# Both directions of a pair's inverses on four quarters of TensorE, and products of zeros in the first stretch of the mixers

## The reference

```python
h = rmsnorm(x) * (1 + sc1) + sh1;  x = x + 0.5 * gt1 * swiglu(h)
h = rmsnorm(x) * (1 + sc2) + sh2;  x = x + gt2 * mix(h)      # GLA | Hyena | RWKV-7
h = rmsnorm(x) * (1 + sc3) + sh3;  x = x + 0.5 * gt3 * swiglu(h)
```

```python
def step(state, inp):                      # one token
    r_t, w_t, k_t, v_t, a_t, b_t = inp
    sa = einsum('bhvk,bhk->bhv', state, a_t)
    state = state * w_t[:, :, None, :] + sa[..., None] * b_t[:, :, None, :] + v_t[..., None] * k_t[:, :, None, :]
    return state, einsum('bhvk,bhk->bhv', state, r_t)
```

## Time and profile before

| what | us |
|---|---|
| median of 3 executions | 2027.83 |
| lowest and highest | 2014.14, 2028.31 |
| the profiled execution | 2029.15 |
| its span, first to last instruction | 2027.2 |
| TensorE busy | 1910.2 (94%) |
| VectorE, ScalarE, GpSimd busy | 1095.8, 739.1, 33.2 |
| layer 0: first and second mixer stage | 478.7 to 600.5, 601.4 to 723.2 |
| layer 1: the same | 1459.1 to 1578.3, 1579.1 to 1695.0 |

### The profile page before, as it was taken

One profiled execution on the slowest core, in us unless ns is written; L12 is line 12 of the kernel. 1 busy time (PEld: TensorE's weight loads), 2 busy tenths in 40 slices (PEclk: granted clock), 3 DMA queues, 4 the chain that ended last, 5 costly groups with the idle time before them and its releaser, 6 DMA issues. The chain is left out here.

```text
span 2027.2 us, 38671 instructions
## 1 busy us (share of the span) xinstructions
PE 1910.2 (94%) x16360; PEld 1748.5 (86%) x16360; DVE 1095.8 (54%) x1845; ACT 739.1 (36%) x1108; POOL 33.2 (2%) x62
## 2 busy tenths in 40 slices
PE   5999999998888989999999999999978898999997
PEld 2888999995665879999999999999747497999997
DVE  3544444865537466554455554476564756655533
ACT  3333333435224244333343333344441424433322
POOL 0000000000001000000000000000000100000000
PEclk9999999998789999999999999999979798999999
DMA  7766233423446233333343333442240401333332
GB/s 271 263 224 222 90 129 137 158 101 113 142 129 212 85 109 125 124 124 113 127 145 124 124 118 114 138 169 90 87 148 4 159 13 66 125 124 124 105 128 89
DMA packets 73192, 263.25 MB, mean 130 GB/s; under 512 B 9696, under 2 KB 10848, under 8 KB 56928
## 3 DMA queue, kind: packets, MB, share of 16 engines
q1 hardware_dynamic: 73056, 261.27, 37.9%
HBM read 259.08 MB, written 2.16 MB: 129 GB/s over the span
## 5 line engine op out<-in xcount | busy, mean ns | idle before, releaser
L157 PE MATMUL ps<-h_head,w_head 128*128 128x386 f32 x1824 | 624.0, 342 | 9.2 <-DVEq L243 4.1
L157 PE MATMUL ps<-h_head,w_rest 128*128 128x386 f32 x1824 | 619.3, 340 | 0.0
L157 PE MATMUL ps<-h_rest,w_head 128*128 128x386 f32 x1824 | 617.3, 338 | 0.0
L219 ACT ACTIVATE w_head<-w_raw 128x2048 fp32r<-128x2048 f32 (+1 forms) x176 | 303.0, 1721 | 609.2 <-PE ps L157 598.9
L222 DVE TENSOR_TENSOR w_rest<-w_raw,w_head 128x2048 fp32r<-128x2048 f32 (+1 forms) x176 | 360.7, 2049 | 204.4 <-ACT w_head L219 204.3
L157 PEld LDWEIGHTS ps<-h_head,w_head 128*128 128x128 f32 x1824 | 345.9, 190 | 28.6 <-issue 18.8
L157 PEld LDWEIGHTS ps<-h_head,w_rest 128*128 128x128 f32 x1824 | 345.8, 190 | 0.0
L157 PEld LDWEIGHTS ps<-h_rest,w_head 128*128 128x128 f32 x1824 | 343.0, 188 | 0.2
L157 PE MATMUL ps<-gu_head,w_head 128*128 128x384 f32 x832 | 279.9, 336 | 11.4 <-DVE gu_rest L813 11.4
L157 PE MATMUL ps<-gu_rest,w_head 128*128 128x384 f32 x832 | 279.4, 336 | 0.0
L157 PE MATMUL ps<-gu_head,w_rest 128*128 128x384 f32 x832 | 279.3, 336 | 0.0
(11 more groups left out here) (294 smaller groups left out, 1798.1 us busy)
## 6 DMA issues: line engine op xcount, KB each, us to landing
w_raw<-in_w_in SPq DMA_DIRECT2D x88, 1024.0 KB, 4.8
w_raw<-in_w_out SPq DMA_DIRECT2D x64, 704.0 KB, 4.0
w_raw<-in_ada_w SPq DMA_DIRECT2D x41, 1024.0 KB, 6.2
ada_raw<-in_ada_w SPq DMA_DIRECT2D x31, 1024.0 KB, 6.4
w_raw<-in_mix_in SPq DMA_DIRECT2D x26, 1024.0 KB, 4.9
w_raw<-in_mix_out SPq DMA_DIRECT2D x8, 1024.0 KB, 5.0
hyena_const<-in_hconst SPq DMA_DIRECT2D x2, 1792.0 KB, 9.6
x<-in_x_in SPq DMA_DIRECT2D x1, 1536.0 KB, 12.2
```

The lines of the kernel that those rows point to most:

```text
L157: return nc.tensor.matmul(out, lhsT, rhs, start=start, stop=stop)
L219: return nc.scalar.activation(self.HI[src], self.RAW[src], ACT.Copy)
```

## The change

The inverse is built otherwise. With J for identity plus something: X2 and D2 (`s1`, for each z), then T1 = J2·T, X4, T2 = J4·T, X8, and INV = J8·T; then Q is its transpose, EX = ET·INV and G its transpose form, Y1 = JE·Q, EX2 from G and EX, and Y = JG·Y1. `crossed` issues both directions together: direction 0 writes the partitions it reads, direction 1 the other half, into two neighbouring banks, so that four quarters of the array are used, and an eviction takes both banks, 768 columns, at once. Because the halves are crossed once more by `straight`, the heads are back in place at the end. The banks of each pair change to 0, 1, 2, 3 and 4, 5, 6, 7.

`keep_busy` multiplies a tile of zeros with the identity and adds to bank 7, in the first mixer stage at three places. The orders of both stages are written anew on every engine; in the two-pair stage `B` and `A` go in step. The waits of the modulation units change: the second set's first unit waits for B's `y1` too.

The diff, cut to its core:

```diff
+                self.X, self.T = (self.XQ[:, :, :, x, :] for x in range(2))
+                self.D4, self.X4, self.J8 = self.D, self.D2, self.X
+                self.INV, self.Q, self.EX, self.JE, self.G = self.J2, self.T, self.D, self.J4, self.X
+                self.Y1, self.JG, self.Y = self.D2, self.ET, self.J4
...
+            def crossed(self, ba, bb, lhsT, rhs):
+                for c in range(NCH):
+                    for h in range(2):
+                        mm(bank(ba, TOK)[half(h), c * C:c * C + C], lhsT[half(h), 0, c, :], rhs[half(h), 0, c, :])
+                    for h in range(2):
+                        last = mm(bank(bb, TOK)[half(1 - h), c * C:c * C + C], lhsT[half(h), 1, c, :], rhs[half(h), 1, c, :])
                 return last
...
+            def straight(self, ba, bb, lhsT, rhs):
+                for z, b in enumerate((ba, bb)):
+                    for c in range(NCH):
+                        for h in range(2):
+                            last = mm(bank(b, TOK)[half(h), c * C:c * C + C], lhsT[half(h), z, c, :], rhs[half(h), z, c, :])
+                return last
...
+            def pe_d4(self, pe):
+                self.after_act(pe, "d2_1")
+                self.after_dve(pe, "x2_1")
+                self.pe_step(self.crossed(*self.even(), self.X, self.D2), "d4")
+            def pe_t1(self, pe):
+                self.after_dve(pe, "j2_1")
+                self.after_pool(pe, "q1")
+                self.pe_step(self.crossed(*self.odd(), self.J2, self.T), "t1")
+            def pe_x4(self, pe):
+                self.after_act(pe, "d4")
+                self.pe_step(self.crossed(*self.even(), self.D2, self.X), "x4")
+            def pe_t2(self, pe):
+                self.after_dve(pe, "j4")
+                self.after_act(pe, "t1")
+                self.pe_step(self.crossed(*self.odd(), self.J4, self.T), "t2")
+            def pe_x8(self, pe):
+                self.after_dve(pe, "x4")
+                self.pe_step(self.crossed(*self.even(), self.D4, self.X4), "x8")
+            def pe_t(self, pe):
+                self.after_dve(pe, "j8")
+                self.pe_step(self.straight(*self.odd(), self.J8, self.T), "t")
+            def pe_q(self, pe):
+                self.after_act(pe, "t_0")
+                self.after_dve(pe, "t_1")
+                for c in range(NCH):
+                    for h in range(2):
+                        mm(bank(self.b0, TOK)[half(h), c * C:c * C + C], self.INV[half(h), 0, c, :], cst("istack", 0, None, 64 * h, 64 * h + 64))
+                    for h in range(2):
+                        last = mm(bank(self.b1, TOK)[half(1 - h), c * C:c * C + C], self.INV[half(h), 1, c, :],
+                                  cst("istack", 0, None, 64 * h, 64 * h + 64))
+                self.pe_step(last, "q")
+            def pe_ex(self, pe):
+                self.after_act(pe, "t_0")
+                self.after_dve(pe, "t_1")
+                self.pe_step(self.crossed(*self.odd(), self.ET, self.INV), "ex")
+            def pe_g(self, pe):
+                self.after_act(pe, "q")
+                self.pe_step(self.crossed(*self.even(), self.INV, self.ET), "gm")
+            def pe_y1(self, pe):
+                self.after_act(pe, "q")
+                self.after_dve(pe, "ex")
+                self.pe_step(self.crossed(*self.odd(), self.JE, self.Q), "y1")
+            def pe_ex2(self, pe):
+                self.after_act(pe, "gm")
+                self.after_dve(pe, "ex")
+                self.pe_step(self.crossed(*self.even(), self.G, self.EX), "ex2")
...
+            def pe_y(self, pe):
+                self.after_dve(pe, "jg")
+                self.after_act(pe, "y1")
+                self.pe_step(self.straight(*self.even(), self.JG, self.Y1), "y")
...
+            def act_both(self, act, name, out, banks):
+                self.after_pe(act, name)
+                self.act_step(nc.scalar.activation(out, self.both(banks), ACT.Copy), name)
+            def act_d4(self, act):
+                self.after_pool(act, "q1")
+                self.act_both(act, "d4", self.D4, self.even())
...
+            def dve_one_plus(self, dve, product, out, banks, name):
+                self.after_pe(dve, product)
+                ones = cst("istack").unsqueeze(1).unsqueeze(1).to_broadcast([128, 2, NCH, C])
+                self.tt(out, self.both(banks), ones, ALU.add, name)
+            def dve_one_plus_x4(self, dve):
+                self.dve_one_plus(dve, "x4", self.J4, self.even(), "j4")
+            def dve_x4(self, dve):
+                self.after_pe(dve, "x4")
+                self.dve_step(nc.vector.tensor_copy(self.X4, self.both(self.even())), "x4")
...
-                A = Pair(scope, SEMS[0:5], lay, 0, (0, 1, 2), 6, PR, TG, AL, MO)
-                G = Gla(scope, SEMS[5:10], lay, (3, 4, 5), P, MO)
+                A = Pair(scope, SEMS[0:5], lay, 0, (0, 1, 2), 3, PR, TG, AL, MO)
+                G = Gla(scope, SEMS[5:10], lay, (4, 5, 6), P, MO)
                 ADA = Ada(scope, SEMS[10:15], 2, [7] * sets, 1)
                 bias_done = SEMS[15]
+                zero = sb(scope, "zero", [128, 128])
+                def keep_busy(pe, n):
+                    A.after_pool(pe, "identity")
+                    for _ in range(n):
+                        mm(bank(7, 128), zero[:, :], cst("ident"), False, False)
...
+                    keep_busy(pe, 9)
                     ada_products(pe, 0, 4)
                     A.pe_nat(pe, 1)
                     ada_products(pe, 0, 5)
+                    keep_busy(pe, 7)
                     A.pe_gram(pe, 0, 0)
                     ada_products(pe, 0, 6)
+                    keep_busy(pe, 5)
...
-                A = Pair(scope, SEMS[0:5], lay, 1, (0, 1, 2), 6, PR, TG, AL, MO)
-                B = Pair(scope, SEMS[5:10], lay, 2, (3, 4, 5), 6, PR, TG, AL, MO, (A.act_done, A.AC["s6_1"]))
+                A = Pair(scope, SEMS[0:5], lay, 1, (0, 1, 2), 3, PR, TG, AL, MO)
+                B = Pair(scope, SEMS[5:10], lay, 2, (4, 5, 6), 7, PR, TG, AL, MO, (SEMS[16], 1))
...
+                            pe.wait_ge(B.act_done, B.AC["y1"])
```

More of the change, by code:

```diff
@@ L1492, in pe_gram, with even, odd, both @@
                 self.pe_step(last, f"gram{z}{b}")
-            def each(self, b, lhsT, rhs):
-                for c, e in PROBS:
-                    last = mm(bank(b, TOK)[half(e), c * C:c * C + C], lhsT(c, e), rhs(c, e))
-                return last
-            def power(self, z):
-                return lambda c, e: self.XQ[half(e), z, c, 0, :]
-            def q(self, z):
-                return lambda c, e: self.XQ[half(e), z, c, 1, :]
-            def of(self, buf, z):
-                return lambda c, e: buf[half(e), z, c, :]
+            def crossed(self, ba, bb, lhsT, rhs):
[4 more added lines that the diff above has]
+                        last = mm(bank(bb, TOK)[half(1 - h), c * C:c * C + C], lhsT[half(h), 1, c, :], rhs[half(h), 1, c, :])
+                return last
+            def straight(self, ba, bb, lhsT, rhs):
[4 more added lines that the diff above has]
+                return last
+            def even(self):
+                return self.b0, self.b1
+            def odd(self):
+                return self.b2, self.b3
+            def both(self, banks):
+                ba, bb = banks
+                assert bb == ba + 1
+                return PS[:, ba * 512:bb * 512 + 512].rearrange("p (z x) -> p z x", x=512)[:, :, 0:TOK].rearrange("p z (c t) -> p z c t", t=C)
+            def one_of(self, banks, z):
+                return bank(banks[z], TOK).rearrange("p (c t) -> p c t", t=C)
             def pe_s1(self, pe, z):
-                ba, bb = self.pair_banks(z)
                 self.after_act(pe, "bt12")
@@ new lines, in pe_s1 @@
+                for b, lhsT, rhs in ((ba, self.X, self.D), (bb, self.D, self.X)):
+                    for c in range(NCH):
+                        for h in range(2):
+                            last = mm(bank(b, TOK)[half(h), c * C:c * C + C], lhsT[half(h), z, c, :], rhs[half(h), z, c, :])
+                self.pe_step(last, f"s1_{z}")
+            def pe_d4(self, pe):
+                self.after_act(pe, "d2_1")
+                self.after_dve(pe, "x2_1")
+                self.pe_step(self.crossed(*self.even(), self.X, self.D2), "d4")
@@ L1818, in dve_power_q @@
-            def dve_power_q(self, dve, z):
-                ba, bb = self.pair_banks(z)
-                self.after_pe(dve, f"s2q_{z}")
-                spans = [(0, ba, 2)] if bb == ba + 1 else [(0, ba, 1), (3, bb, 1)]
-                for first, b, n in spans:
-                    products = PS[:, b * 512:b * 512 + n * 512].rearrange("p (b x) -> p b x", b=n)[:, :, 0:TOK]\
-                        .rearrange("p b (c x t) -> p b c x t", c=3, x=2)
-                    xq = self.XQ[:, z, first:first + 3 * n, :, :].rearrange("p (b c) x t -> p b c x t", b=n)
-                    nc.vector.tensor_copy(xq[:, :, :, 0, :], products[:, :, :, 0, :])
```

(9 more changed lines are left out.)

580 lines of the change are left out of this document (262 added, 318 removed).

## The result

The changed kernel takes 2038.9 us (median of 7 runs, 2037.5 to 2045.9), the kernel before 2020.9 in seven runs beside it (2014.1 to 2028.3): a ratio of 1.0081, interval 1.0063 to 1.0099. It is slower by 0.8%, and 25 us above the forecast of 2014. The profiled executions took 2037.51 us (span 2035.7) and 2029.15; they are 8.4 us apart where the medians are 18.

The account below looks back on a forecast made before the run. Bounds: TensorE in inverses and chunk loops, VectorE early in the two-pair stage, a falling clock early in the first stage. 2029.15 - 8.5 - 2.7 - 3.0 = 2015.0, less 1.3 for the median: 2014 us; range 2000 to 2032.

Parts of the forecast that it names:

- a crossed step of both directions (48 records) is 0.98 us: Inverse on four quarters: 20.5 ns a record, against 1.40 us for two single steps; 2.8 us of TensorE saved a pair.
- rival 3: Inverse: four-quarter products run at 14.6 ns, or overlap of two pairs hides more than allowed; 2006 us, chance 0.21.
- Rival 2: Inverse: quarters do not overlap beyond the diagonal, 29 ns a record instead of 20.5; +25 us, 2039, chance 0.07.
- Theory 1: From the experiments, not the prediction: TensorE's instructions come in blocks of 128 records, one in some 3.5 us; faster products wait.
- Two pairs, -3.0: Two-pair stages, both pairs in step: later inverse start, shorter inverse; +0.2 us in layer 0, -3.2 in layer 1.
- First stage, -2.7: First mixer stages: chunk loops no longer carry two units and four transposes, 1.2 us in layer 0; layer 1 gains 1.5.
- Zeros, -8.5: First mixer stages: products of zeros keep the clock up, first inverse product 4.5 us sooner in layer 0, 4 in layer 1.
- rival 1: First mixer stages: the clock falls despite the zeros; 8.5 us not won, +1.5 us a layer; 2025 us, chance 0.24.
- The base: Whole kernel: terms summed against the profiled execution of 2029.15 us, with 1.3 us taken off at the end for the median.

## Why the prediction was wrong

**The step that failed** is "a crossed step of both directions (48 records) is 0.98 us" as a price that adds up. I costed the inverse by the duration of its products alone: 18.2 us a pair before, 15.4 after. In the traces, where no gap lies between, a crossed step starts 0.75 to 0.86 us behind the last in the first stage and 0.70 in the two-pair stage, the low bound, as rival 3 had it. Rival 2 is refuted. So is, for these products, the rule that I set beside it from the page "TensorEngine Tiling (Array Packing)" of the Trainium skill, that different row tiles can't access one PSUM bank at the same time: four quarters at 14.6 to 16.3 ns a record are nearly twice as fast as one diagonal. Yet the result is the time that rival 2 gives, 2039, by another cause; that it fits is luck. The count of records went from 576 a pair to 672, and at 27 to 29 ns a record, the pace of the supply (3.5 to 3.7 us a block), 672 are 18.1 to 19.5 us: no less than before. Theory 1 gives the two pairs' 1344 records 36 to 39 us, and they took 37.2 and 38.1, where I had 33.0 and 32.0. No row of before could warn of it: 29 ns is one diagonal's own pace (460 records at 29.6 ns without a gap, in the run of two quarters beside the loads), and it lies just above the supply's 27.

Of the two traces' 22.6 us against the forecast (8.4 more where I had 14.2 less), 13.1 are in the two-pair stages, 8.6 in the first ones, 0.8 ahead of them.

**Two pairs, -3.0:** they took 4.3 and 5.8 us more. The start of the inverse was right in layer 1, 51.4 us into the stage where 52.1 was forecast, and 3.4 us sooner than forecast in layer 0, 51.1 for 54.5 (whose sum I had also added up 1 us short: 618 + 22.6 + 0.4 + 3.1 is 644.1, not 643). Against before it came 4.4 and 5.8 us later (layer 0, layer 1), about what the stages lost. It was to be paid back by the shorter inverse, and nothing of that came in layer 1, 3.2 us of it in layer 0. The chunk loops in step were a second term too small: 29.7 us for my 25.9 in layer 0 and 23.4 for my 20.5 in layer 1, nearly the 24.0 of before. What holds them was not looked into.

**First stage, -2.7:** mechanism right in layer 1, where the second chunk step came 37.7 us after the first product for a forecast of 37.4. In layer 0 it came after 45.3 us, not 39.5, with 4.3 us of gaps without a reason beside the weight loads. In all, the kernel with the new first stage, its early unit and no zeros is 0.12% slower than before, with an interval that reaches down to 0.01%, and not faster.

**Zeros, -8.5:** the first inverse product came 3.0 us sooner in layer 0 where I had 4.5, and 0.2 in layer 1 where I had 4. The zeros hold the clock from 20.5 to 39.4 us into the stage, but I had it stay up behind that too. In the 20.6 us that follow it is 0.82 for 0.55 before in layer 0, and 0.58 in both kernels in layer 1: there rival 1, the clock falling all the same, is true. I also left out that 42 more records shift every border behind them, which beside the old inverse cost 4.5 us in the two-pair stage, and that the early unit costs 0.2%, which I had put into the same figure.

**The base.** I took 1.3 us off for the median. In seven runs the median of before was 2020.9, 8.2 under its profiled execution, and in later groups 2024.3 to 2027.6. My range stood on a high execution; this alone moves the forecast to about 2007 and makes the miss larger, not smaller.

**Left open.** The zeros gain 0.38% beside the new two-pair stage and nothing beside the old: shifted borders and loads are candidates, since without zeros the first layer's two-pair stage took 137.5 us for 130.1, more in each of its first three parts. And the first layer's first stage took 122.8, 124.4 and 129.6 us in three kernels that share its code, with mean clocks of 0.90, 0.88 and 0.83. In them the clock first rose 7, 19 and 20 us into the stage, ahead of all zeros; I can only say that these vary together, and that a single trace's first stage can't price a change of a few us.

A page of the Trainium skill bears on the cause: "Runtime: NRT & Kernel Launch", section Instruction fetch mechanics, says that instructions come in 16 KiB blocks of 256, which q8's packets agree with, and that crossing a border is mostly hidden because the engine dispatches more slowly than the fills. For the old order the traces agree: it has one such gap, of 0.7 us. For the four quarters they don't: 256 instructions went in 2.09 us, and the next came 1.37 us after their end, 3.46 us after their start.

## What to carry over

Count instructions as well as microseconds: a stretch of small products has two prices, their duration and the pace at which their instructions arrive, and work made denser than that only turns busy time into gaps that no engine is named for. If a trace shows such gaps, count the records between them; if the count is constant, use fewer and wider products. Longer ones put between the short ones ran almost free here, but moving units that were there already gained nothing. Anything added to a stream moves the borders for all that follows, so compare stages that the edit did not touch before judging it, and try adding in whole blocks.

## What the hardware showed

A new block of 128 records every 3.46 us in a quiet core, 3.31 at the least in any trace and 3.63 in the median. A gap's end 2.16 to 2.90 us behind the start of an instruction packet, 116 times of 116. Four quarters at 14.6 to 16.3 ns a record with 64 columns and 28.1 with 128; one diagonal at 29 to 29.6, two that take turns at 24. No packet of instructions for 3.5 to 3.9 us while weight loads filled the queues, three times. Products of 8 columns that were no cheaper than wide ones of the same tile: 112 ns a record for 128x128 where 128 columns took 107, and 58 for 64x64 on one quarter; 43 of 128x128 by 8 were dearer than the 64 small ones that replaced them.
